# GpSimd computes twelve of the weight residues of a two-block transformer kernel

## The chip, the cores and the metric

The kernel runs on one core of a Trainium2 chip, as one program and one launch. The metric is the device time of that program in microseconds (us): 1126.8 us, the median of three runs (1125.76 to 1127.77). A core has five engines with a queue each: TensorE (PE in the rows, its weight loads PEld), VectorE (DVE), ScalarE (ACT), GpSimd (POOL) and SyncE (SP), which here only issues transfers. They work out of one on-chip memory, SBUF; the results of matmuls lie in PSUM.

## The reference, cut to what matters

Two transformer blocks follow each other on 256 rows of 1,024 features, all in float32.

```python
def first_block(x, c, ...):
    sh_m, sc_m, g_m, sh_f, sc_f, g_f = split(silu(c) @ w_ada + b_ada, 6)
    h = modulate(rmsnorm(x, norm_mix_g), sh_m, sc_m)
    q, k, v, qi, ki, wi, u, ga, gb = split(h @ w_in, split_at)
    y_attn = dsa_attention(q, k, v, qi, ki, wi) @ w_attn_proj   # top 64 keys of each row
    y_conv = conformer_conv(u, w_dw, b_dw, ln_g, ln_b) @ w_conv_proj   # 31 taps, layernorm, silu
    merged = sigmoid(ga) * y_attn + sigmoid(gb) * y_conv
    x = x + g_m * (merged @ w_out)
    a, b = split(modulate(rmsnorm(x, norm_ffn_g), sh_f, sc_f) @ w_ffn_in, 2)
    return rmsnorm(x + g_f * ((silu(a) * b) @ w_ffn_out))

def second_block(x, mem, ...):   # two attentions, cross attention to mem, feed forward
    ...
```

## The kernel before, in words

**Every product with a weight is three matmuls.** The fast float32 form of TensorE keeps fewer bits than float32, so each weight w is used as w_hi + w_lo and each activation a as a_hi + a_lo, and a product is a_hi·w_hi + a_hi·w_lo + a_lo·w_hi (`mm3`, lines 455 to 457). The weights come from memory in blocks of 1 MB into four `raw_weights` buffers (`RAW`); a block holds two *pieces* of 128x1024. For every piece ScalarE writes `w_hi` (a copy with rounding, line 909), then the residue `w_lo` = raw − w_hi is computed by VectorE (line 1223), then TensorE runs 12 matmuls of 512 columns with it. `w_hi` and `w_lo` are rings of four pieces (`RING`). The whole kernel has 277 pieces, numbered in the order of use.

**What orders a piece.** All order is written by hand: every engine runs its own list, and semaphores count. ScalarE counts `hi_ready` for each w_hi, and starts piece q when TensorE has used piece q − 4 (`piece_used`). VectorE waits for `hi_ready` ≥ q + 1 and counts `lo_ready`. TensorE waits for `lo_ready` ≥ q + 1 (`piece`, line 461 on). SyncE loads block b when `lo_ready` says that both pieces of block b − 4 are done (`load`).

**The stretch in question** holds pieces 45 to 72:

- Pieces 45 to 48 are the second slab of the first gate `ga`. Beside them VectorE runs the top-64 search: 8 rounds of `max` and `match_replace` for each half of the rows, one tap of the 31-tap convolution behind each of those (`conv_taps`, line 1407), and a residue behind every second round (pieces 45 to 52).
- Pieces 49 to 56 are the gate `gb`. Their matmuls stand inside the 16 steps of the attention, one piece in every second step (`second_gate`). A step of VectorE is a bias tile (line 1456), scores plus bias with their maximum (line 1443), its negation (line 1447), six taps, and in the odd steps from 5 on a residue (pieces 53 to 58). ScalarE takes the exponentials and turns the next w_hi. Behind the last step come the residues of pieces 59 and 60, and then the division of the attention's output (lines 1476 and 1484), the layernorm of the convolution (lines 1493 to 1557, with one small GpSimd operation, line 434) and its silu.
- Pieces 57 to 64 are the two projections of attention and convolution (`P_PA`, `P_PC`), each in two halves of the columns; VectorE multiplies their results by the gates (`gated_first` line 1514, `gated_second` lines 1522 and 1525), with two residues ahead of each such group. Pieces 65 to 72 are the output projection (`P_OUT1`).

**GpSimd** issues the transfers of `w_ada` until 162 us, each when VectorE has used the buffer (`ada_block`), and computes small reciprocal roots (`rstd`, lines 419, 434 and 444). Between 162 and 363 us it has the one operation of line 434.

## Time and profile before

| what | value |
|---|---|
| device time, median of 3 runs | 1126.8 us |
| span of the profiled execution | 1126.1 us |
| TensorE busy | 967.9 us (86%) |
| VectorE busy | 659.0 us (59%) |
| ScalarE busy | 475.3 us (42%) |
| GpSimd busy | 27.6 us (2%) |

The profile is of one execution, whose span from the first to the last instruction is 1126.1 us, 0.7 us (0.06%) below the median of the runs. The page also gives the busy share of each engine in 40 slices of 28 us. In most of them TensorE is at nine or more tenths; in the slices from 197 to 310 us, where the search and the attention lie, it falls to 8, 7, 8 and 6 while VectorE is at 8 and 9. Durations are from the first to the last cycle of an instruction; on VectorE an instruction starts some 0.08 us before the one in front of it has ended, so the distance of two starts is the cost of an instruction in a queue.

### The profile page before, as it was taken

How to read it: one execution, taken by the hardware profiler on the slowest of the kernel's cores; microseconds unless marked ns; L12 is line 12 of the kernel's file. 1: busy time of each engine (PE TensorE's matmuls, PEld its weight loads, DVE VectorE, ACT ScalarE, POOL GpSimd, SP SyncE). 2: the span in 40 equal slices, each digit the busy share in tenths (PEclk: the TensorE clock that was granted, in tenths of full speed). 3: DMA queues.
4: the chain of work that ended last, by engine and by line, in shares of the span. 5: the costliest groups of instructions: out<-in, count | busy, mean ns of one | idle time of the engine just before them, and what ended most of it. 6: DMA issues, size and time to landing. Idle time of an engine off the chain costs nothing.

```text
span 1126.1 us, 12350 instructions
## 1 busy us (share of the span) xinstructions
PE 967.9 (86%) x4205; PEld 785.5 (70%) x4205; DVE 659.0 (59%) x1074; ACT 475.3 (42%) x704; POOL 27.6 (2%) x40
## 2 busy tenths in 40 slices
PE   1998998968786999989949979876888989999896
PEld 1877886745675788878838856655677778888785
DVE  1975986899665455546655563444745355555443
ACT  3524543324434444433334434543435345555341
POOL 1110110000000000000000000000000000000000
PEclk9996996878889899999969968888999989999998
DMA  9793992412244455555714621222544044555440
GB/s 345 279 324 103 376 367 74 135 38 76 75 150 149 155 183 186 186 186 190 271 62 156 199 93 48 102 75 74 168 150 148 3 150 150 186 186 186 149 150 38
DMA packets 101541, 178.01 MB, mean 158 GB/s; under 512 B 5222, under 2 KB 51419, under 8 KB 101498
## 3 DMA queue, kind: packets, MB, share of 16 engines
q1 hardware_dynamic: 94682, 151.23, 40.6%
q0 software_dynamic: 6816, 26.22, 6.5%
q8 instruction: 25, 0.41, 0.1%
q14 instruction: 18, 0.15, 0.0%
HBM read 176.39 MB, written 1.05 MB: 158 GB/s over the span
## 4 chain that ended last, share of the span: by engine, by line
PE 52%; issue 26%; DVE 12%; ACT 5%; DMA 4%; SPq 0%; POOL 0%; DVEq 0%; POOLq 0%; ACTq 0%
PE bank L455 12%; PE bank L456 12%; PE bank L457 12%; PE bank L752 5%; DMA ada_raw<-in_w_ada 2%; DVE w_lo L1223 2%; DVE conv_out L1407 2%; ACT w_hi L909 2%; DVE ada_acc L1286 2%; DMA tap_rows<-in_w_dw 1%; PE bank L624 1%; PE bank L496 1%; PE bank L598 1%; PE bank L517 1%; PE bank L860 1%
## 5 line engine op out<-in xcount | busy, mean ns | idle before, releaser
L1223 DVE TENSOR_TENSOR w_lo<-raw_weights,w_hi 128x1024 fp32r<-128x1024 f32 x277 | 338.3, 1222 | 323.1 <-ACT w_hi L909 322.4
L909 ACT ACTIVATE w_hi<-raw_weights 128x1024 fp32r<-128x1024 f32 x277 | 292.5, 1058 | 413.0 <-PE bank L457 335.0
L455 PE MATMUL bank<-w_hi,a_hi 128*128 128x512 f32 (+1 forms) x944 | 390.0, 413 | 24.5 <-DVE a_lo L1738 6.0
L456 PE MATMUL bank<-w_lo,a_hi 128*128 128x512 f32 (+1 forms) x944 | 381.8, 404 | 0.0
L457 PE MATMUL bank<-w_hi,a_lo 128*128 128x512 f32 (+1 forms) x944 | 381.2, 404 | 0.0
L455 PEld LDWEIGHTS bank<-w_hi,a_hi 128*128 128x128 f32 x944 | 189.0, 200 | 71.8 <-issue 30.6
L457 PEld LDWEIGHTS bank<-w_hi,a_lo 128*128 128x128 f32 x944 | 187.9, 199 | 40.6
L456 PEld LDWEIGHTS bank<-w_lo,a_hi 128*128 128x128 f32 x944 | 188.9, 200 | 37.5
L1286 DVE SCALAR_TENSOR_TENSOR ada_acc<-ada_raw,row_stats,ada_acc 128x512 f32<-128x512 f32 (+1 forms) x84 | 62.9, 749 | 6.6 <-DMA ada_raw<-in_w_ada 4.8
L752 PE MATMUL bank<-w_hi,ff_hi 128*128 128x512 f32 x176 | 56.2, 401 | 6.3 <-DVE hidden_rows L1579 3.2
L752 PE MATMUL bank<-w_lo,ff_hi 128*128 128x512 f32 x176 | 55.5, 397 | 0.0
L752 PE MATMUL bank<-w_hi,ff_lo 128*128 128x512 f32 x176 | 55.4, 396 | 0.0
L1407 DVE SCALAR_TENSOR_TENSOR conv_out<-conv_in,conv_taps_T,conv_out 128x256 f32<-128x256 f32 x120 | 50.8, 475 | 0.0
L752 PEld LDWEIGHTS bank<-w_hi,ff_hi 128*128 128x128 f32 x176 | 33.4, 191 | 14.4 <-DVE hidden_rows L1579 3.6
L752 PEld LDWEIGHTS bank<-w_lo,ff_hi 128*128 128x128 f32 x176 | 33.9, 193 | 7.2
L752 PEld LDWEIGHTS bank<-w_hi,ff_lo 128*128 128x128 f32 x176 | 33.9, 192 | 7.2
L1056 ACT ACTIVATE probabilities_T<-bank 128x128 f32<-128x128 f32 (+1 forms) x32 | 10.6, 330 | 39.8 <-PE bank L633 39.8
L517 PE MATMUL bank<-constants,z_projected 128*128 128x128 f32 x88 | 17.1, 368 | 11.3 <-DVE z_projected L1646 3.9
L506 PE MATMUL bank<-constants,x_residual 128*128 128x128 f32 x48 | 9.8, 390 | 18.8 <-DVE x_residual L1622 12.7
L1443 DVE CUSTOM_DVE_ANT_0 masked_scores<-bank,bias_tile 128x128 f32<-128x128 f32 (+1 forms) x32 | 11.5, 358 | 24.4 <-issue 12.4
L413 POOL DMA_DIRECT2D ada_raw<-in_w_ada x24 | 18.1, 757 | 303.4 <-DVE ada_acc L1286 294.7
L1048 ACT ACTIVATE probabilities<-masked_scores,row_stats 128x128 f32<-128x128 f32 (+1 forms) x32 | 14.4, 450 | 25.9 <-DVE row_stats L1447 25.7
(218 smaller groups left out, 699.3 us busy)
## 6 DMA issues: line engine op xcount, KB each, us to landing
raw_weights<-in_w_in SPq DMA_DIRECT2D x40, 1024.0 KB, 5.1
ada_raw<-in_w_ada POOLq DMA_DIRECT2D x24, 1024.0 KB, 6.4
raw_weights<-in_w_ffn_in SPq DMA_DIRECT2D x44, 512.0 KB, 4.3
raw_weights<-in_w_gate_up SPq DMA_DIRECT2D x44, 512.0 KB, 4.3
raw_weights<-in_w_ffn_out SPq DMA_DIRECT2D x9, 1024.0 KB, 5.0
raw_weights<-in_w_down SPq DMA_DIRECT2D x9, 1024.0 KB, 5.0
raw_weights<-in_w_ckv SPq DMA_DIRECT2D x8, 1024.0 KB, 11.4
raw_weights<-in_w_out SPq DMA_DIRECT2D x8, 1024.0 KB, 5.0
```

The lines of the kernel that those rows point to most:

```text
L413: pool.dma_start(ada_raw[:, n % 2, :].rearrange("p (k n) -> p k n", k=4), slab_src(w2["w_ada"], 4 * k, s)).then_inc(ada_landed[n % 2], 16)
L455: pe.matmul(ps, hi[:, kt, ts], wh, start=start, stop=False)
L456: pe.matmul(ps, hi[:, kt, ts], wl, start=False, stop=False)
L457: return pe.matmul(ps, lo[:, kt, ts], wh, start=False, stop=stop)
L517: last = pe.transpose(bank[b0 + g][:, kk * SEQ + t * P:kk * SEQ + (t + 1) * P], src[:, t, c:c + P], ident)
L752: last = pe.matmul(bank[2 * t + c][:], lhs[:, kt, ts], w[:, c * W:(c + 1) * W], start=(kt == 0 and n == 0), stop=(kt == KF - 1 and n == 2))
L909: act.activation(w_hi[:, q % RING, 0:m], raw[:, b % RAW, half * PIECE:half * PIECE + m], ACT.Copy)\
L1048: act.activation(p_work[:, n % 2, 0, 0:keys], s_work[:, n % 2, 0, 0:keys], ACT.Exp, bias=stat[:, 34 + n % 2:35 + n % 2], accum_out=stat[:, ...
L1223: dve.tensor_tensor(w_lo[:, q % RING, 0:m], raw[:, b % RAW, half * PIECE:half * PIECE + m], w_hi[:, q % RING, 0:m], ALU.subtract).then_inc ...
L1286: o = dve.scalar_tensor_tensor(out=slot, in0=w, scalar=c, in1=slot, op0=ALU.mult, op1=ALU.add)
L1407: dve.scalar_tensor_tensor(out=conv_out[:, g, :], in0=conv_in[:, g, k:k + SEQ], scalar=taps[:, g, k:k + 1], in1=conv_out[:, g, :], op0=ALU ...
L1443: dve.tensor_tensor_reduce(s_work[:, n % 2, 0, 0:keys], bank[4 + n % 2][:, 0:keys], bias, DH ** -0.5, -3e38, ALU.add, ALU.max, stat[:, 32 ...
```

## The change

`POOL_LO` is a list of twelve pieces: 46, 48, 50, 52, 54, 56, 58, 60, 62, 64, 66 and 68. VectorE leaves their residues out; GpSimd computes them, each when `hi_ready` says that w_hi is there, and counts a semaphore of its own, `pool_lo`. Whoever waits for a residue (TensorE's `piece`, SyncE's `load`) waits for `pool_lo` for these pieces and for `lo_ready` for all others, whose counts are lower by the pieces that were left out before them. A block of which one piece is GpSimd's has two waits ahead of its load. For that the loads of blocks 21 to 28 are written out in place of a loop. The subtraction itself, its operands and the rings are the same.

```diff
+POOL_LO = tuple(range(P_IN1 + 29, P_OUT1 + 4, 2))
+
+def lo_before(p):
+    return p - sum(q < p for q in POOL_LO)
...
+    def lo_event(p):
+        return (pool_lo, POOL_LO.index(p) + 1) if p in POOL_LO else (lo_ready, lo_before(p) + 1)
...
             if b >= RAW:
-                sp.wait_ge(lo_ready, last_piece_of(b - RAW) + 1 + i * step)
+                q = last_piece_of(b - RAW)
+                if q in POOL_LO or q - 1 in POOL_LO:
+                    sp.wait_ge(*lo_event(q - 1))
+                    sp.wait_ge(*lo_event(q))
+                else:
+                    sp.wait_ge(lo_ready, lo_before(q) + 1 + i * step)
...
+        def residue(q):
+            b, half = block_of(q)
+            pool.wait_ge(hi_ready, q + 1)
+            pool.tensor_tensor(w_lo[:, q % RING, :], raw[:, b % RAW, half * PIECE:(half + 1) * PIECE],
+                               w_hi[:, q % RING, :], ALU.subtract).then_inc(pool_lo, 1)
+        for q in POOL_LO:
+            if q < P_PC:
+                residue(q)
         pool.wait_ge(sem["ln_var"], 1)
         pool.tensor_tensor(stat[:, 62:64], ..., ALU.pow).then_inc(sem["ln_rstd"], 1)
+        for q in POOL_LO:
+            if q >= P_PC:
+                residue(q)
         rstd(N_H2)
...
         def piece(p, u, j, n, i=0, ...):
-            pe.wait_ge(lo_ready, p + 1 + i * 8)
+            ready_sem, count = lo_event(p)
+            pe.wait_ge(ready_sem, count + i * 8)
...
         def conv(p, n=1, i=0):        # VectorE
             for q in range(p, p + n):
+                if q in POOL_LO:
+                    continue
```

**VectorE in the top-64 search.** `MAX` and `MATCH_REPLACE` are the two steps of a round, and `conv_out<-conv_in,conv_taps_T,conv_out` is a tap. Before, a residue stands behind every second round:

```order
L1423 MATCH_REPLACE score<-top_75,score 128x256 [waits top_step]
L1407 SCALAR_TENSOR_TENSOR conv_out<-conv_in,conv_taps_T,conv_out 128x256 [waits conv_done]
L1223 TENSOR_TENSOR w_lo<-raw_weights,w_hi 128x1024 [waits hi_ready]
L1420 MAX top_75<-score 128x8 [waits top_step]
L1407 SCALAR_TENSOR_TENSOR conv_out<-conv_in,conv_taps_T,conv_out 128x256 [waits conv_done]
```

Now, where the piece is GpSimd's:

```order
L1458 MATCH_REPLACE score<-top_75,score 128x256 [waits top_step]
L1442 SCALAR_TENSOR_TENSOR conv_out<-conv_in,conv_taps_T,conv_out 128x256 [waits conv_done]
L1455 MAX top_75<-score 128x8 [waits top_step]
L1442 SCALAR_TENSOR_TENSOR conv_out<-conv_in,conv_taps_T,conv_out 128x256 [waits conv_done]
L1458 MATCH_REPLACE score<-top_75,score 128x256 [waits top_step]
```

The residue and its wait for `hi_ready` are gone between the two rounds; four of the eight residues of the search go in this way (pieces 46, 48, 50 and 52).

**The end of the attention, VectorE and GpSimd.** `RECIPROCAL` and the two operations behind it divide the attention's output. VectorE before:

```order
L1407 SCALAR_TENSOR_TENSOR conv_out<-conv_in,conv_taps_T,conv_out 128x256 [waits conv_done] x2
L1223 TENSOR_TENSOR w_lo<-raw_weights,w_hi 128x1024 [waits hi_ready] x3
L1476 RECIPROCAL row_stats<-row_stats 128x16 [waits attention_exp]
L1484 TENSOR_TENSOR z_projected<-bank,row_stats 128x512 [waits attention_pv,attention_recip]
L1484 TENSOR_TENSOR z_projected<-bank,row_stats 128x512
L1493 TENSOR_TENSOR conv_out<-conv_out,bank 128x1024 [waits ln_mean]
```

VectorE now:

```order
L1442 SCALAR_TENSOR_TENSOR conv_out<-conv_in,conv_taps_T,conv_out 128x256 [waits conv_done] x2
L1258 TENSOR_TENSOR w_lo<-raw_weights,w_hi 128x1024 [waits hi_ready]
L1511 RECIPROCAL row_stats<-row_stats 128x16 [waits attention_exp]
L1519 TENSOR_TENSOR z_projected<-bank,row_stats 128x512 [waits attention_pv,attention_recip]
L1519 TENSOR_TENSOR z_projected<-bank,row_stats 128x512
L1528 TENSOR_TENSOR conv_out<-conv_out,bank 128x1024 [waits ln_mean]
```

GpSimd before, from the last issue of `w_ada` of the loop on:

```order
L413 DMA ada_raw<-in_w_ada 128x4x512
L429 REGISTER_ALU
L429 COMPARE_AND_BRANCH
L434 TENSOR_TENSOR row_stats<-row_stats,constants 128x2 [waits ln_var]
L419 TENSOR_TENSOR row_stats<-row_stats,constants 128x2 [waits norm_mean]
```

GpSimd now:

```order
L432 DMA ada_raw<-in_w_ada 128x4x512
L448 REGISTER_ALU
L448 COMPARE_AND_BRANCH
L456 TENSOR_TENSOR w_lo<-raw_weights,w_hi 128x1024 [waits hi_ready] x8
L463 TENSOR_TENSOR row_stats<-row_stats,constants 128x2 [waits ln_var]
L456 TENSOR_TENSOR w_lo<-raw_weights,w_hi 128x1024 [waits hi_ready] x4
L438 TENSOR_TENSOR row_stats<-row_stats,constants 128x2 [waits norm_mean]
```

Of the three residues ahead of the division (58, 59, 60) one stays (59). GpSimd has eight residues ahead of the layernorm's small operation, which stands in a queue behind the one of piece 60, and four behind it.

**VectorE at the second gating.** Before, with the two halves of the columns:

```order
L1223 TENSOR_TENSOR w_lo<-raw_weights,w_hi 128x1024 [waits hi_ready] x2
L1522 TENSOR_TENSOR z_projected<-bank,z_projected 128x512 [waits piece_used]
L1525 TENSOR_TENSOR z_projected<-z_projected 128x512 [waits acc0_free]
L1522 TENSOR_TENSOR z_projected<-bank,z_projected 128x512
L1525 TENSOR_TENSOR z_projected<-z_projected 128x512 [waits acc1_free]
```

Now:

```order
L1258 TENSOR_TENSOR w_lo<-raw_weights,w_hi 128x1024 [waits hi_ready]
L1557 TENSOR_TENSOR z_projected<-bank,z_projected 128x512 [waits piece_used]
L1560 TENSOR_TENSOR z_projected<-z_projected 128x512 [waits acc0_free]
L1557 TENSOR_TENSOR z_projected<-bank,z_projected 128x512
L1560 TENSOR_TENSOR z_projected<-z_projected 128x512 [waits acc1_free]
```

One residue in place of two stands ahead of each group (65 ahead of the first half, 67 ahead of the second).

## Rows read from the trace of the kernel before

**Rows 1.** The page: the span, and busy time of each engine.

```profile
span 1126.1 us, 12350 instructions
PE 967.9 (86%) x4205; PEld 785.5 (70%) x4205; DVE 659.0 (59%) x1074; ACT 475.3 (42%) x704; POOL 27.6 (2%) x40
```

**Rows 2.** Windows: busy us (instructions) by engine, granted clock, DMA share, GB/s.

```profile
215.20:231.00 15.80, 7.35 (x33) 5.75 (x32) 15.71 (x41) 5.43 (x6) 0.00 (x0) 0.80 0.26 77
231.00:291.00 60.00, 49.52 (x200) 36.21 (x200) 57.07 (x164) 24.04 (x60) 0.00 (x0) 0.82 0.16 55
291.00:303.00 12.00, 7.50 (x38) 6.57 (x37) 6.87 (x11) 5.54 (x7) 0.71 (x1) 0.73 0.43 158
```

**Rows 3.** The page's costliest groups: count, busy us, mean ns, idle before, releaser.

```profile
L1223 DVE TENSOR_TENSOR w_lo<-raw_weights,w_hi 128x1024 fp32r<-128x1024 f32 x277 | 338.3, 1222 | 323.1 <-ACT w_hi L909 322.4
L909 ACT ACTIVATE w_hi<-raw_weights 128x1024 fp32r<-128x1024 f32 x277 | 292.5, 1058 | 413.0 <-PE bank L457 335.0
L1407 DVE SCALAR_TENSOR_TENSOR conv_out<-conv_in,conv_taps_T,conv_out 128x256 f32<-128x256 f32 x120 | 50.8, 475 | 0.0
```

**Rows 4.** Timeline of the search's second half: start us, us, engine, what.

```profile
215.22 1.22 DVE L1223 TENSOR_TENSOR w_lo<-raw_weights,w_hi 128x1024 fp32r<-128x1024 f32 x1 [3.30 <-ACT w_hi L909]
216.36 0.42 DVE L1420 MAX8 top<-score 128x8 f32<-128x256 f32 x1
216.70 0.47 DVE L1407 SCALAR_TENSOR_TENSOR conv_out<-conv_in,conv_taps_T,conv_out 128x256 f32<-128x256 f32 x1
...
217.21 1.06 ACT L909 ACTIVATE w_hi<-raw_weights 128x1024 fp32r<-128x1024 f32 x1 [2.02 <-PE bank L457]
...
231.01 1.61 PE L624 MATMUL bank<-kT,qT 64*128 64x128 f32 x4 [8.46 <-DVE modulation_T L1373]
```

**Rows 5.** Timeline inside the attention, VectorE and TensorE.

```profile
258.70 1.22 DVE L1223 TENSOR_TENSOR w_lo<-raw_weights,w_hi 128x1024 fp32r<-128x1024 f32 x1
...
275.33 0.29 DVE L1443 CUSTOM_DVE_ANT_0 masked_scores<-bank,bias_tile 128x128 f32<-128x128 f32 x1
...
266.65 0.69 PE L633 MATMUL bank<-constants,probabilities 128*128 128x128 f32 x2 [2.67 <-ACT probabilities L1048]
...
273.58 0.48 PE L624 MATMUL bank<-kT,qT 64*128 64x128 f32 x2
```

**Rows 6.** Timeline of the attention's end, VectorE and TensorE.

```profile
291.83 1.23 DVE L1223 TENSOR_TENSOR w_lo<-raw_weights,w_hi 128x1024 fp32r<-128x1024 f32 x1 [1.30 <-ACT w_hi L909]
293.26 1.29 DVE L1484 TENSOR_TENSOR z_projected<-bank,row_stats 128x512 f32<-128x512 f32 x2
295.71 1.22 DVE L1496 TENSOR_TENSOR conv_sq<-conv_out 128x1024 f32<-128x1024 f32 x1
...
290.49 0.78 PE L640 MATMUL bank<-z_projected,probabilities_T 128*128 128x64 f32 x6
...
302.21 1.19 PE L691 MATMUL bank<-conv_sq,constants 128*128 128x256 f32 x2 [1.65 <-DVE conv_sq L1505]
```

**Rows 7.** Timeline of the second gating, VectorE, ScalarE and TensorE.

```profile
322.57 1.23 DVE L1223 TENSOR_TENSOR w_lo<-raw_weights,w_hi 128x1024 fp32r<-128x1024 f32 x1 [1.50 <-ACT w_hi L909]
...
328.01 1.22 DVE L1223 TENSOR_TENSOR w_lo<-raw_weights,w_hi 128x1024 fp32r<-128x1024 f32 x1 [0.43 <-ACT w_hi L909]
...
326.92 1.06 ACT L909 ACTIVATE w_hi<-raw_weights 128x1024 fp32r<-128x1024 f32 x1 [1.66 <-PE bank L457]
...
331.95 1.97 PE L704 MATMUL bank<-constants,z_projected 128*128 128x128 f32 x8 [4.25 <-DVE z_projected L1525]
```

**Rows 8.** Groups of instructions: count, busy us, mean ns, idle before, releaser.

```profile
L419 POOL TENSOR_TENSOR row_stats<-row_stats,constants 128x2 f32<-128x2 f32 x8 | 5.6, 702 | 455.6 <-DVE row_stats L1231 450.3 <-DMA constants<-shape_constants 5.3
...
L1447 DVE TENSOR_SCALAR row_stats<-row_stats 128x1 f32<-128x1 f32 x32 | 4.9, 154 | 1.2 <-DVE row_stats L1443 0.2
...
L1235 DVE TENSOR_SCALAR scaled_rows<-x_residual,row_stats 128x1024 f32<-128x1024 f32 x1 | 0.8, 753 | 0.8 <-POOL row_stats L419 0.8
...
L1525 DVE TENSOR_TENSOR z_projected<-z_projected 128x512 f32<-128x512 f32 x8 | 5.5, 692 | 0.3
```

More of the change, by code:

```diff
@@ L224, in build @@
     hi_ready, lo_ready, piece_used = S("hi_ready"), S("lo_ready"), S("piece_used")
+    pool_lo = S("lo_by_gpsimd")
+    def lo_event(p):
+        return (pool_lo, POOL_LO.index(p) + 1) if p in POOL_LO else (lo_ready, lo_before(p) + 1)
     acc_free = [S("acc0_free"), S("acc1_free")]
@@ L344, in _ @@
                 load(13 + j, slab_src(w2["w_in"], 4 * (j % 2), i * (2 * W) + (j // 2) * W), None, i, 8)
-        with sp.Fori(0, 2) as i:
-            for j in range(4):
-                load(21 + j, slab_src(w2["w_in"], 4 * (j % 2), i * (2 * W) + (C_GA + (j // 2) * W)), None, i, 8)
+        for s in range(4):
+            for j in range(2):
+                load(21 + 2 * s + j, slab_src(w2["w_in"], 4 * j, C_GA + s * W))
         sp.dma_start(final_g[:], a["norm_final_g"].partition_broadcast(P)).then_inc(final_landed, 16)
@@ L552, in _ @@
         turn(N_H1, xs_z)
-        pe.wait_ge(lo_ready, P_SMALL + 1)
+        pe.wait_ge(*lo_event(P_SMALL))
         for t in range(TT):
@@ L744, in feed_forward @@
                     reduce_gate(8 * 12, gate_slot).then_inc(sem["ada_reduced"], 1)
-                pe.wait_ge(lo_ready, p + kt + 1)
+                pe.wait_ge(*lo_event(p + kt))
                 pe.wait_ge(*after(tag, "hidden_lo", kt // 2 + 1))
```

## The prediction

> **What bounds the kernel now.** I read the page first: TensorE is busy for 86% of 1126.1 us and VectorE for 59% [rows 1], so over the whole kernel taking work from VectorE buys nothing: w_lo has 323.1 us of idle time before it, nearly all of it waiting for ScalarE's w_hi [rows 3], and w_hi in turn waits for TensorE. The windows show where that is otherwise. From 215.2 us, where VectorE's last wait in the search ends, to 231.0 VectorE is busy for 15.71 of 15.80 us and TensorE for 7.35; from 231 to 291, in the attention, VectorE is busy for 57.07 of 60 us [rows 2]. The timeline says the same from the other side: TensorE's first scores at 231.01 had waited 8.46 us for VectorE [rows 4]. So from 215 to 293 us the list of VectorE is the path. From 303 to 326.7 TensorE runs without a gap and nothing is to be had, and at 331.95 it has waited 4.25 us for the second gating [rows 7]. What the change is worth is read from these places alone.
>
> **What is taken from VectorE.** Twelve residues of 1.22 us [rows 3], 14.7 us of busy time; in a queue one costs the distance of two starts, 216.36 − 215.22 = 1.14 us [rows 4]. Piece by piece:
> - 46, 48, 62 and 64 lie where VectorE waits anyway: ahead of 215.22 it had stood idle for 3.30 us until TensorE had used piece 45 [rows 4]. Nothing is gained, and a delay of VectorE by up to 3.3 + 2 × 1.14 = 5.6 us ahead of 215 is covered.
> - 50 and 52, in the second half of the search: 2 × 1.14 = 2.3 us, all on the path. The rounds need no w_hi, and that of piece 51 is there early enough.
> - 54 and 56 lie behind the steps of the attention: 2.3 us. What is late next is TensorE: the scores for the step of 275.33 were ready at 273.58 + 0.48 = 274.06, 1.27 us ahead of it, while TensorE itself had stood for 2.67 us at 266.65 waiting for the exponential, which moves with VectorE [rows 5]. I take 2.0 us, with 1.3 and 2.3 as ends.
> - 58 and 60 at the end. Behind 58 VectorE stood idle, so its absence there frees nothing. 60 starts at 291.83, after 1.30 us of waiting for its w_hi, and the division starts at 293.26. Without it the division waits for the attention's last matmuls, over at 290.49 + 0.6 = 291.1, and for its reciprocal, 0.3 us: 291.4, a gain of 1.85 us, handed through the layernorm to TensorE at 302.21 [rows 6].
> - 66 and 68: without 66 (322.57) the first half of the gating starts when TensorE has used piece 62, some 2 us earlier; the second half then waits for piece 64, used at 326.92 (ScalarE's w_hi is released by it), and not for the residue of 68, which ends at 328.01 + 1.14 = 329.15 [rows 7]. That is 329.15 − 326.95 = 2.2 us of the 4.25.
>
> Together 2.3 + 2.0 + 1.85 + 2.2 = 8.3 us, if GpSimd's work is free.
>
> **What is put on GpSimd.** The trace has no operation of this size on it. Its nearest row, 128x2, takes 702 ns where VectorE takes 154 for 128x1 [rows 8]; by that factor of 4.6 a residue would take 5.6 us, which is the upper end, and 1.22, VectorE's own, is the lower. I take 2.4, twice VectorE's, for an engine that reads its two operands one after the other; ScalarE passes one operand of this size in 1.06 [rows 3], and two such passes are 2.1. As a price from a page alone: the Trainium skill (GPSIMD Engine Reference, Performance versus the Vector engine) gives 4,497 ns for a float32 `tensor_tensor` of 2,048 elements, which would be an estimate of 2.25 us here and change the sum by under 1 us.
>
> At 2.4 us nobody waits for the result itself. In the projections w_hi of piece q ends 1.1 us after TensorE has used piece q − 4, and three pieces of 2.72 us lie between (the distance of two w_hi there, 1.06 + 1.66 [rows 7]): 8.2 − 1.1 = 7.1 us for the residue. In the search and the attention the distance is longer. The small operation of the layernorm stands behind piece 60's residue, which is over 5 us ahead of it. SyncE's two waits per block are eight pieces ahead of the use. The loads written out without a loop cost nothing: its queue waits on residues.
>
> **What it costs VectorE.** This decides the case, and no row shows it: nowhere does GpSimd read SBUF beside a VectorE operation with two operands there. What rows do show is that VectorE with one operand of 128x1024 in SBUF takes 0.753 us and with two 1.22 [rows 3, 8]. With one operand it goes at twice the rate per element, so a second way into SBUF exists, and two operands fill both. If GpSimd reads through one of them, the two engines must take turns whenever VectorE has two operands in SBUF, and that is a tap (0.475 us, 120 of them [rows 3]), a bias tile and a residue: most of the stretch. The bounds: no hold at all, or the whole 2.4 us of GpSimd's operation less what VectorE has to do meanwhile with one operand. I put turn-taking ahead, for the doubled rate is what a shared second way would look like. The Trainium skill (SBUF — State Buffer, Who interferes with whom) states this outright: a VectorE instruction with two SBUF inputs contends with a GpSimd instruction that reads SBUF, and the later one is blocked until the first has finished. By that rule the sum is the one that follows, and without it 8.3 us are gained.
>
> The sum with turns:
> - 50 and 52: each holds the next tap for 2.4 less a `MAX` or `MATCH_REPLACE` of 0.35, against 1.14 saved: 2 × (2.05 − 1.14) = +1.8.
> - 54 and 56: 2.4 less up to 0.75 of one-operand work (scores and negation), so 1.65 to 2.4 against 1.14: +0.5 to +1.3 each; I take +0.9, so +1.8.
> - 58: its w_hi comes in the taps ahead of the last step, so it holds them for nothing to 2.4, and nothing is saved there: +1.2.
> - 60: the division reads one operand from PSUM and goes on; the square at 295.71 [rows 6], two operands, loses some 0.4: −1.85 + 0.4 = −1.4.
> - 66 and 68: the operations of line 1525 have two operands in SBUF (0.692 us [rows 8]) and meet both: of the 2.2 us some 0.5 is left, −0.5.
> - 46, 48, 62 and 64: held inside idle time, 0.
>
> +1.8 + 1.8 + 1.2 − 1.4 − 0.5 = **+2.9 us**, a span of 1129.0 and, with the 0.7 between span and median, 1129.7. With the friendly end of each term the sum is 0, with the other +6.
>
> **The rivals.**
> - *Side by side.* The engines read without touching each other. Then the price is 0 and all of 8.3 us stays: 1118.5, between 1116.5 and 1120.5 with the ends of the attention term and with TensorE's clock, which was granted at 0.82 of full in the attention [rows 2] and may rise a little when it waits less. For it speaks that a row that would contradict it is missing; against it the doubled rate. This is the case of the other side; it decides from the point where a residue holds VectorE for under about 74% of what I assume (8.3 of 11.2 us), as with an operation of under 2.0 us.
> - *GpSimd waits for gaps.* VectorE's taps follow without a pause, and GpSimd gets in only at scores, `MAX` and idle time. Then the holds are at their friendly ends and gain and loss cancel: 1126.8, from 1125 to 1128.5.
> - *The long operation.* Turns, and a residue of 5.6 us: five holds on the path each 3.2 us longer, 16 us more: about 1145. Above 5.4 us (two pieces of 2.72) GpSimd would also fall behind TensorE in the projections. Nothing but the factor of tiny operations speaks for it.
>
> **How the numbers follow.** Turns 0.56, of which 0.35 slower by over 0.2% (2.3 us, about what a measurement of this kernel can tell from no change), 0.20 within and 0.01 faster; side by side 0.33, faster; gaps 0.06, within; long operation 0.05, slower. Faster 0.34, same 0.26, slower 0.40. The range has to reach both main cases, 1117.5 to 1133; outside it lie the long operation and the tails of the two. The likeliest case's own range is 1126.5 to 1133.
>
> **What would show it.** A residue of GpSimd of 2.2 to 2.6 us when nothing is beside it. With turns, taps or `MAX`-separated taps that last, or stand, 1.5 to 2.4 us longer exactly once per GpSimd residue, the first scores at about 232.8 in place of 231.01, and the division at about 296; side by side, taps all at 0.475, the first scores near 228.7 and the division near 287. In both, the wait of 4.25 ahead of TensorE's turn of the second half shrinks: to 2.0 side by side, to about 3.8 with turns. From 340 us on the rest should be the same with a shift. The prediction is wrong if taps keep their length beside a GpSimd residue, if that residue takes under 2 us, or if TensorE is seen waiting for `pool_lo`.

## The result, and the profile after

The changed kernel takes 1130.7 us (median of 5 runs, 1129.3 to 1131.2) against 1126.6 us for the kernel before (5 runs, 1124.7 to 1127.8). The ratio is 1.0032, with an interval of 1.0018 to 1.0045: slower by 4.1 us, where 2.9 were forecast. The engines take turns.

The page of the changed kernel answers to [rows 1]. Its group lines give count, busy us, mean ns, idle time ahead and its releaser:

```profile
span 1128.4 us, 12333 instructions
PE 965.2 (86%) x4205; PEld 783.3 (69%) x4205; DVE 660.9 (59%) x1062; ACT 474.7 (42%) x704; POOL 58.0 (5%) x52
...
L1258 DVE TENSOR_TENSOR w_lo<-raw_weights,w_hi 128x1024 fp32r<-128x1024 f32 x265 | 323.7, 1223 | 318.0 <-ACT w_hi L942 317.4
...
L456 POOL TENSOR_TENSOR w_lo<-raw_weights,w_hi 128x1024 fp32r<-128x1024 f32 x12 | 30.5, 2539 | 136.1 <-ACT w_hi L942 136.1
```

VectorE has twelve instructions less, 323.7 us of residues in place of 338.3, and yet it is busy for 1.9 us *more*. So its other instructions grew by 14.6 + 1.9 = 16.5 us. The group of the taps, from 190 to 340 us, says which:

```profile
L1442 DVE SCALAR_TENSOR_TENSOR conv_out<-conv_in,conv_taps_T,conv_out 128x256 f32<-128x256 f32 x120 | 63.8, 583 | 0.0
```

Before, the same 120 took 50.8 us [rows 3]: 13.0 us more. Most of the rest, 2.9 us, is in two additions of the second gating, shown below. The timeline of the search shows one of them, VectorE and then GpSimd (start us, us, engine, what):

```profile
213.25 1.22 DVE L1258 TENSOR_TENSOR w_lo<-raw_weights,w_hi 128x1024 fp32r<-128x1024 f32 x1
...
215.18 0.41 DVE L1458 MATCH_REPLACE8 score<-top,score 128x256 f32<-128x256 f32 x1
215.51 2.23 DVE L1442 SCALAR_TENSOR_TENSOR conv_out<-conv_in,conv_taps_T,conv_out 128x256 f32<-128x256 f32 x1
217.66 0.41 DVE L1455 MAX8 top<-score 128x8 f32<-128x256 f32 x1
```

```profile
214.99 2.46 POOL L456 TENSOR_TENSOR w_lo<-raw_weights,w_hi 128x1024 fp32r<-128x1024 f32 x1 [7.52 <-ACT w_hi L942]
```

`MATCH_REPLACE`, with one operand in SBUF, passes beside GpSimd in its usual 0.41 us. The tap behind it begins at 215.51 and ends at 217.74, 0.29 us after GpSimd has ended (214.99 + 2.46 = 217.45). Without GpSimd it takes 0.47.

An operand in PSUM does not meet GpSimd either. The residue of piece 60 lies beside the division's multiplications and the first step of the layernorm, each with one operand in SBUF and one in PSUM (`bank`), and the latter takes its usual 1.22 us (GpSimd and VectorE):

```profile
297.26 2.37 POOL L456 TENSOR_TENSOR w_lo<-raw_weights,w_hi 128x1024 fp32r<-128x1024 f32 x1 [8.47 <-ACT w_hi L942]
...
298.46 1.22 DVE L1528 TENSOR_TENSOR conv_out<-conv_out,bank 128x1024 f32<-128x1024 f32 x1 [0.42 <-PE bank L702]
```

In the attention, one step's six taps (2.45 us before) and the last step's taps, with the step between on which VectorE waits for scores (the row names the bias tile, but that was over 0.75 us earlier; TensorE's scores ended at 276.04):

```profile
252.12 4.53 DVE L1442 SCALAR_TENSOR_TENSOR conv_out<-conv_in,conv_taps_T,conv_out 128x256 f32<-128x256 f32 x6
...
276.53 0.29 DVE L1478 CUSTOM_DVE_ANT_0 masked_scores<-bank,bias_tile 128x128 f32<-128x128 f32 x1 [0.74 <-DVE bias_tile L1491]
...
284.53 4.54 DVE L1442 SCALAR_TENSOR_TENSOR conv_out<-conv_in,conv_taps_T,conv_out 128x256 f32<-128x256 f32 x6
```

The end of the attention, TensorE and then VectorE, answers to [rows 6]:

```profile
290.75 0.69 PE L666 MATMUL bank<-constants,probabilities 128*128 128x128 f32 x2 [4.41 <-ACT probabilities L1081]
...
292.51 0.63 PE L487 MATMUL bank<-w_hi,a_hi 128*128 128x512 f32 x1
...
295.87 0.78 PE L673 MATMUL bank<-z_projected,probabilities_T 128*128 128x64 f32 x6
```

```profile
292.83 1.23 DVE L1258 TENSOR_TENSOR w_lo<-raw_weights,w_hi 128x1024 fp32r<-128x1024 f32 x1 [1.98 <-ACT w_hi L942]
293.98 0.25 DVE L1511 RECIPROCAL row_stats<-row_stats 128x16 f32<-128x16 f32 x1
296.75 1.29 DVE L1519 TENSOR_TENSOR z_projected<-bank,row_stats 128x512 f32<-128x512 f32 x2 [2.53 <-PE bank L673]
```

The residue of piece 60 is gone, and still the division starts 3.5 us later than before: it waits 2.53 us for TensorE, which is late by the attention, and whose piece 56 takes 4.8 us in place of 2.8. And the second gating, VectorE and TensorE [rows 7]:

```profile
326.10 2.18 DVE L1560 TENSOR_TENSOR z_projected<-z_projected 128x512 f32<-128x512 f32 x1
...
330.21 0.69 DVE L1560 TENSOR_TENSOR z_projected<-z_projected 128x512 f32<-128x512 f32 x1
...
331.54 2.12 DVE L1560 TENSOR_TENSOR z_projected<-z_projected 128x512 f32<-128x512 f32 x1
```

```profile
333.71 1.97 PE L737 MATMUL bank<-constants,z_projected 128*128 128x128 f32 x8 [3.39 <-DVE z_projected L1560]
```

**By stages.** From such rows every profiled execution was cut at five points: (a) VectorE starts the residue of piece 49, (b) TensorE starts the first scores, (c) the maximum of the attention's last step is read, (d) the division starts, (e) TensorE starts the turn of the second half, then the end of the span. Distances in us:

| kernel | a to b | b to c | c to d | d to e | e to end |
|---|---|---|---|---|---|
| before | 15.79 | 55.50 | 6.75 | 38.69 | 794.2 |
| changed | 17.03 | 59.51 | 6.96 | 36.96 | 794.7 |
| e_search | 17.39 | 55.45 | 8.34 | 38.68 | 794.2 |
| e_attn | 15.80 | 59.54 | 8.36 | 38.50 | 794.3 |
| e_end | 15.79 | 55.53 | 4.90 | 38.57 | 792.2 |
| e_noread | 13.53 | 53.13 | 6.33 | 37.16 | 790.2 |
| e_beside0 | 15.79 | 55.52 | 6.75 | 38.71 | 794.2 |
| e_beside1 | 17.02 | 57.87 | 9.04 | 39.01 | 794.3 |
| e_beside2 | 19.72 | 61.80 | 6.76 | 40.65 | 791.7 |
| e_quarters | 14.63 | 57.72 | 6.16 | 35.47 | 791.7 |
| e_early | 17.02 | 59.59 | 4.22 | 38.69 | 792.4 |
| e_reorder | 15.79 | 55.52 | 4.90 | 37.15 | 794.0 |
| e_both | 15.79 | 55.52 | 2.64 | 36.45 | 789.4 |
| e_both_quarters | 14.81 | 55.40 | 2.75 | 37.15 | 787.6 |

The first two columns repeat to 0.2 us wherever the kernels agree there (0.4 for e_search, whose list from a to b is the changed kernel's), and they carry the argument. The last column differs by some 4 us between kernels that are alike behind (e) (all but the last three), so a whole time is read from the runs and not from one profile. Two profiled executions lie well off their kernel's median: that of e_search took 1135.2 us (8.4 above it), that of e_quarters 1119.0 (4.2 below it).

### The profile page after: what moved, and what is told of

Its sections match the earlier page's. It is cut to its first block, busy times and chain, and to the rows that moved or that the text cites. A ratio compares the mean times of both kernels' runs of the same rounds, so it can differ in the third digit from the quotient of the medians.

```text
span 1128.4 us, 12333 instructions
## 1 busy us (share of the span) xinstructions
PE 965.2 (86%) x4205; PEld 783.3 (69%) x4205; DVE 660.9 (59%) x1062; ACT 474.7 (42%) x704; POOL 58.0 (5%) x52
## 4 chain that ended last, share of the span: by engine, by line
PE 52%; issue 24%; DVE 14%; ACT 5%; DMA 4%; POOL 1%; SPq 0%; DVEq 0%; POOLq 0%; ACTq 0%
PE bank L487 13%; PE bank L488 12%; PE bank L489 12%; PE bank L785 5%; DVE conv_out L1442 3%; DMA ada_raw<-in_w_ada 3%; DVE w_lo L1258 2%; ACT w_hi L942 2%; DVE ada_acc L1321 2%; DMA tap_rows<-in_w_dw 1%; PE bank L657 1%; PE bank L529 1%; PE bank L550 1%; PE bank L631 1%; PE bank L893 1%
## 5 line engine op out<-in xcount | busy, mean ns | idle before, releaser
L1258 DVE TENSOR_TENSOR w_lo<-raw_weights,w_hi 128x1024 fp32r<-128x1024 f32 x265 | 323.7, 1223 | 318.0 <-ACT w_hi L942 317.4
L1442 DVE SCALAR_TENSOR_TENSOR conv_out<-conv_in,conv_taps_T,conv_out 128x256 f32<-128x256 f32 x120 | 63.8, 583 | 0.0
L456 POOL TENSOR_TENSOR w_lo<-raw_weights,w_hi 128x1024 fp32r<-128x1024 f32 x12 | 30.5, 2539 | 136.1 <-ACT w_hi L942 136.1
L432 POOL DMA_DIRECT2D ada_raw<-in_w_ada x24 | 18.1, 756 | 302.9 <-DVE ada_acc L1321 294.2
L666 PE MATMUL bank<-constants,probabilities 128*128 128x128 f32 x48 | 13.4, 339 | 16.6 <-ACT probabilities L1081 16.4
L438 POOL TENSOR_TENSOR row_stats<-row_stats,constants 128x2 f32<-128x2 f32 x8 | 5.6, 702 | 426.2 <-DVE row_stats L1266 420.7
```

The source lines that it names most:

```text
L432: pool.dma_start(ada_raw[:, n % 2, :].rearrange("p (k n) -> p k n", k=4), slab_src(w2["w_ada"], 4 * k, s)).then_inc(ada_landed[n % 2], 16)
L456: pool.tensor_tensor(w_lo[:, q % RING, :], raw[:, b % RAW, half * PIECE:(half + 1) * PIECE], w_hi[:, q % RING, :], ALU.subtract).then_inc( ...
L666: last = pe.transpose(bank[6][:, kt * P:(kt + 1) * P], p_work[:, n % 2, 0, kt * P:(kt + 1) * P], ident)
L1258: dve.tensor_tensor(w_lo[:, q % RING, 0:m], raw[:, b % RAW, half * PIECE:half * PIECE + m], w_hi[:, q % RING, 0:m], ALU.subtract).then_inc ...
L1442: dve.scalar_tensor_tensor(out=conv_out[:, g, :], in0=conv_in[:, g, k:k + SEQ], scalar=taps[:, g, k:k + 1], in1=conv_out[:, g, :], op0=ALU ...
```

## The experiments

### Each part alone

```diff
-POOL_LO = tuple(range(P_IN1 + 29, P_OUT1 + 4, 2))
+POOL_LO = (46, 48, 50, 52)          # e_search
+POOL_LO = (54, 56, 58)              # e_attn
+POOL_LO = (60, 62, 64, 66, 68)      # e_end
```

e_search: 

> GpSimd computes the residues of pieces 46, 48, 50 and 52 only; VectorE computes all others. Turns theory: in the search each residue of GpSimd stretches one tap by 1.8 to 1.9 us; the two ahead of the idle time cost nothing, the other two cost 2 x 1.76 and save 2 x 1.14, so the time is 1.2 us above before (+0.1%). Rival, side by side (the loss of the whole change lies elsewhere, for instance in TensorE's clock): 2.3 us below before.

e_attn: 

> GpSimd computes the residues of pieces 54, 56 and 58 only. Turns theory: each stretches the taps by 1.5 to 2.1 us, two save 1.14 each and the third saves nothing, and TensorE, which then waits over 4 us ahead of piece 56, runs that piece at its lower clock (4.8 in place of 2.85 us): 4 to 6 us above before. Without the effect of the clock 3 to 4 us above. Rival, side by side: 2 us below.

e_end: 

> GpSimd computes the residues of pieces 60, 62, 64, 66 and 68 only. Turns theory: piece 60 gives 1.85 less 0.4 us, the gating gives 0.9 us of its 2.2 (one addition in each half is stretched from 0.69 to 2.1 us): 2.3 us below before, faster by 0.2%. Side by side: 4 us below. If GpSimd's residues cost everywhere: at or above before.

Measured, as ratios to the kernel before: e_search 1.0005 (0.9991 to 1.0019), e_attn 1.0046 (1.0033 to 1.0058), e_end 0.9967 (0.9954 to 0.9979): +0.6, +5.2 and -3.7 us, each with about 1.5 us of uncertainty, +2.1 together against +3.6 by the ratio of the whole. In its own stage e_search costs 1.6 us and e_attn 4.0, as the changed kernel does within 0.4. The rest of e_attn's loss lies between (c) and the division (8.36 against 6.75), where TensorE waits 4.83 us and the first half of piece 56 runs at the low clock. By the whole time e_search is not told from no change, while "side by side", 2.3 us below, is outside its interval. In e_end the division comes 1.85 us sooner (6.75 to 4.90), which is the forecast's gain for piece 60 to the digit, since there TensorE's last wait is what it was:

```profile
287.79 0.44 PE L666 MATMUL bank<-constants,probabilities 128*128 128x128 f32 x2 [2.75 <-ACT probabilities L1081]
```

So the change is a gain where VectorE has few two-operand instructions beside the residue, and a loss where the taps follow each other.

### Is it GpSimd's reading?

Three kernels put twelve operations on GpSimd beside the kernel *before*, at the pieces of `POOL_LO`, on data that nobody waits for (two resident operands of 128x1024, one, none):

```diff
+        def beside(q):
+            pool.wait_ge(hi_ready, q + 1)
...
+            pool.tensor_tensor(dst, mem_v[:, :, 0:W], mem_v[:, :, W:2 * W], ALU.subtract)   # e_beside2
+            pool.tensor_scalar(dst, mem_v[:, :, 0:W], 1.0, None, ALU.mult)                  # e_beside1
+            pool.memset(dst, 0.0)                                                           # e_beside0
```

e_beside2: 

> The kernel before with all its residues on VectorE; GpSimd in addition subtracts two 128x1024 operands of resident data into a place that nobody reads, twelve times, at the moments at which it computes a residue in the change. Turns theory: nothing is saved and every hold stays, 2 x 1.8 in the search, 1.5 to 2.1 for each of 54, 56 and 58, about 1.4 for each of 66 and 68, some clock: 11 to 14 us above before (1.0 to 1.2%). Side by side: no difference.

e_beside1: 

> The same with an operation of one operand (a multiplication by 1) in place of two. Turns theory: the taps are held again, each as long as this shorter operation lasts; if it lasts 1.0 to 1.3 us, 3 to 6 us above before. If only two reading streams of GpSimd get in the way: no difference.

e_beside0: 

> The same with an operation that only writes (a fill with zeros). If what is shared is the way in which an engine reads: no tap is stretched and the time is that of before within 0.2%. If any GpSimd operation on SBUF holds VectorE: each tap beside it is stretched by its duration, 3 to 5 us above before.

A fourth is the changed kernel in which GpSimd only fills `w_lo`, so that TensorE's a_hi·w_lo of twelve pieces is that of a constant:

```diff
-            pool.tensor_tensor(w_lo[:, q % RING, :], raw[...], w_hi[:, q % RING, :], ALU.subtract).then_inc(pool_lo, 1)
+            pool.memset(w_lo[:, q % RING, :].bitcast(F32), 0.0).then_inc(pool_lo, 1)
```

e_noread: 

> The change with GpSimd filling w_lo with zeros in place of subtracting: VectorE has the same list as in the change, but GpSimd reads nothing, so the part a_hi times w_lo of these twelve pieces is left out. Turns in reading only: no hold is left and the whole of the gain shows that I worked out for work that is free on GpSimd, 8.3 us below before (0.7%). If the gain was overrated (TensorE or ScalarE next in line): 3 to 6 us below. If writes hold too: near before.

Measured: e_beside2 1.0110 (1.0078 to 1.0143), e_beside1 1.0051 (1.0037 to 1.0064), e_beside0 1.0006 (0.9996 to 1.0016), e_noread 0.9917 (0.9900 to 0.9933), that is +12, +6, +0.7 and -9.3 us. The first, the third and the fourth came as the theory had them; in e_beside1 the time is in the expected range, but the operation lasts 3.34 us in the mean and not 1.0 to 1.3 (last section). The groups between 190 and 340 us, of e_beside2, e_beside0 and e_noread in this order:

```profile
L1419 DVE SCALAR_TENSOR_TENSOR conv_out<-conv_in,conv_taps_T,conv_out 128x256 f32<-128x256 f32 x120 | 64.7, 591 | 0.0
...
L438 POOL TENSOR_TENSOR z_projected<-mem_v 128x1024 f32<-128x1024 f32 x12 | 34.7, 2892 | 138.6 <-ACT w_hi L921 138.6
```

```profile
L1419 DVE SCALAR_TENSOR_TENSOR conv_out<-conv_in,conv_taps_T,conv_out 128x256 f32<-128x256 f32 x120 | 50.9, 476 | 0.0
...
L438 POOL MEMSET z_projected<- 128x1024 f32 x12 | 11.4, 954 | 147.2 <-ACT w_hi L921 147.2
```

```profile
L1442 DVE SCALAR_TENSOR_TENSOR conv_out<-conv_in,conv_taps_T,conv_out 128x256 f32<-128x256 f32 x120 | 50.9, 476 | 0.0
...
L456 POOL MEMSET w_lo<- 128x1024 f32 x12 | 11.4, 954 | 144.3 <-ACT w_hi L941 144.3
```

An operation that reads holds the taps though nobody uses its result, one that only writes does not (476 ns). In e_beside1, where GpSimd reads one operand, the taps take 514 ns in the mean. This shows that the price is the reading, and neither the waits nor the semaphores that the change adds. e_noread is also the rival "side by side" made real: 2.26 us gained in the search and 2.37 in the attention, where 2.3 and 2.0 had been worked out. From (c) to (e), however, it gains 1.95 and not 4.05: half of piece 56 ran at the low clock there too, after a wait of 2.70 us. So the whole, 9.3 against 8.3, is nearer to the forecast than its parts are. The Trainium skill (SBUF — State Buffer, SBUF: two separate sides) has it that the two engines lock a shared pair of ports for a whole instruction, VectorE with two SBUF inputs only against a GpSimd operation that reads. The four runs agree on who holds whom. On "for a whole instruction" the two-operand operation agrees and e_beside1 does not: it holds a tap for 0.75 of its 2.77 us.

### Turns by the instruction: the residue in quarters

```diff
-            pool.tensor_tensor(w_lo[:, q % RING, :], raw[...], w_hi[:, q % RING, :], ALU.subtract).then_inc(pool_lo, 1)
+            for c in range(half * PIECE, (half + 1) * PIECE, 256):
+                o = c - half * PIECE
+                pool.tensor_tensor(w_lo[:, q % RING, o:o + 256], raw[:, b % RAW, c:c + 256],
+                                   w_hi[:, q % RING, o:o + 256], ALU.subtract).then_inc(pool_lo, 1)
```

e_quarters: 

> The changed kernel, with every residue of GpSimd written as four operations of 128x256 in place of one of 128x1024. If the two engines take turns by whole instructions, no tap is held for more than about 0.7 us, but four are held for each residue in place of one: the sum of the taps' extra time stays near 9 us or grows by GpSimd's fixed cost, and the time is 0 to +3 us against the changed kernel (ratio to the kernel before 1.003 to 1.006). If a hold came from something that lasts as long as GpSimd has work at all, single taps would still last 2.2 us or more. If the engines shared the way cycle by cycle, the taps would all grow by the same small share, and nothing would change with the size.

Measured: 0.9965 (0.9949 to 0.9981), 1123.2 us. This is 7.5 us *below* the changed kernel, and faster than the kernel before. The expectation was wrong: I had let four short holds add up to one long one. The groups of this kernel between 190 and 340 us, a stretch of the search, and GpSimd and VectorE at the residue of 58:

```profile
L1444 DVE SCALAR_TENSOR_TENSOR conv_out<-conv_in,conv_taps_T,conv_out 128x256 f32<-128x256 f32 x120 | 57.3, 528 | 0.0
L458 POOL TENSOR_TENSOR w_lo<-raw_weights,w_hi 128x256 fp32r<-128x256 f32 x48 | 40.1, 864 | 121.4 <-ACT w_hi L944 121.4
```

```profile
214.52 0.79 DVE L1444 SCALAR_TENSOR_TENSOR conv_out<-conv_in,conv_taps_T,conv_out 128x256 f32<-128x256 f32 x1
215.23 0.08 DVE L1460 MATCH_VALUE_LOAD score<-top,score 128x8 f32 x1
215.31 0.40 DVE L1460 MATCH_REPLACE8 score<-top,score 128x256 f32<-128x256 f32 x1
215.63 0.56 DVE L1444 SCALAR_TENSOR_TENSOR conv_out<-conv_in,conv_taps_T,conv_out 128x256 f32<-128x256 f32 x1
```

```profile
281.35 3.42 POOL L458 TENSOR_TENSOR w_lo<-raw_weights,w_hi 128x256 fp32r<-128x256 f32 x4 [12.01 <-ACT w_hi L944]
...
279.71 2.92 DVE L1444 SCALAR_TENSOR_TENSOR conv_out<-conv_in,conv_taps_T,conv_out 128x256 f32<-128x256 f32 x6
282.55 0.94 DVE L1493 SCALAR_TENSOR_TENSOR bias_tile<-constants,score 128x256 f32<-128x256 f32 x1
...
284.06 1.37 DVE L1444 SCALAR_TENSOR_TENSOR conv_out<-conv_in,conv_taps_T,conv_out 128x256 f32<-128x256 f32 x2
```

GpSimd works longer (40.1 us against 30.5), but the taps grow by 6.5 us in place of 13.0. Between two quarters VectorE gets in, and in the search part of each quarter lies beside `MAX` and `MATCH_REPLACE`. In the attention the four quarters of a residue hold only three instructions, for about 0.5 us each: here a tap in the run of six (2.92 in place of 2.45), the bias tile (0.94 in place of 0.42) and a tap in the run of two (1.37 in place of 0.87); one quarter falls beside the scores, which have one operand in SBUF. That is 1.5 us in place of the 2.08 of a whole residue. Against e_noread, where nothing is held, a whole residue costs (17.03 - 13.53) / 2 = 1.75 us in the search and (59.51 - 53.13) / 3 = 2.13 in the attention, and one in quarters 0.55 and 1.53. VectorE's own costs 1.14. That is the rule of the case: in quarters it pays in the search and not in the attention. By the stages the two stretches with taps account for 4.2 of the 7.5 us below the changed kernel. Another 2.3 lie between (c) and (e): the held additions of the second gating take 1.21 and 1.19 us in place of 2.18 and 2.12, and TensorE's wait at (e) is 2.56 in place of 3.39. Against the kernel before, the stages give 1.2 us won in the search, 2.2 lost in the attention and 3.8 won from (c) to (e), TensorE's clock included.

### TensorE's piece behind the last wait

```diff
             for n in range(len(STEPS)):
+                ahead = between is not None and n == len(STEPS) - 1
+                if ahead:
+                    between(n // 2)
                 turn_p(n)
...
-                if between is not None and n % 2:
+                if between is not None and n % 2 and not ahead:
                     between(n // 2)
```

e_early: 

> The changed kernel, with one difference: TensorE runs the attention's last gate piece (56) ahead of the last step's turn instead of behind it. In the changed kernel TensorE waits 4.41 us ahead of that turn (290.75), then runs piece 56 at the lower of its two clocks until 295.87, and the division waits for it 2.53 us, until 296.75. Theory (the end of the attention lost its gain because the piece stood behind a longer wait): the piece goes into the wait, runs in 2.8 us, the division starts 2.5 us sooner, at about 294.2, where VectorE is free for it, and the time is some 2.5 us below that of the changed kernel (ratio to the kernel before about 1.001). Rival (VectorE's taps and the residue of 59 are what set the division, and TensorE's clock is of no weight): the division stays within 0.5 us of 296.75 and the time with it (ratio about 1.003).

Measured: 1.0009 (0.9998 to 1.0020), 1127.9 us, 2.8 us below the changed kernel. TensorE and VectorE of this kernel:

```profile
291.08 0.44 PE L666 MATMUL bank<-constants,probabilities 128*128 128x128 f32 x2 [1.63 <-ACT probabilities L1084]
```

```profile
294.34 1.29 DVE L1522 TENSOR_TENSOR z_projected<-bank,row_stats 128x512 f32<-128x512 f32 x2
```

From (c) to the division it is 4.22 us in place of 6.96, as expected (the division at 294.34, 294.2 expected), and VectorE waits for nobody there. But the path gives back 1.73 us between the division and (e) (38.69 against 36.96), where TensorE's clock is lower than in the changed kernel: granted at 0.68 of full from 294.3 to 303.7, against 0.82 there. By the profiles the piece's place is thus worth 1 us until (e); by the runs it is 2.6 ± 2.0. That it sets the division is shown; how much of the whole it is worth is not settled closer than that.

### What VectorE can do alone

If the residues on the path are the matter, they can be moved in VectorE's own list to where it waits, without GpSimd. e_reorder does that to the kernel before:

```diff
-        conv(P_IN1 + 42, 2)
+        conv(P_IN1 + 42)
...                                  # behind the a_lo of the attention's output
+        conv(P_IN1 + 43)
...                                  # second gating, in both blocks
-                conv(p2 + 4 + 2 * c, 2)
+                conv(p2 + 4 + 2 * c)
...                                  # behind the addition that ends the half
+                conv(p2 + 5 + 2 * c)
```

e_reorder: 

> No residue on GpSimd. VectorE computes piece 60's residue behind the layernorm's square and the attention's a_lo, and of each pair ahead of the second gating the second one behind it, in both blocks. Theory: what the change gains at these places is the place in VectorE's queue, not the engine: 1.85 + 2.2 us in the first block and 2.2 in the second, 6 us below before (0.5%). Rival: the residues are late for TensorE or ScalarE there and nothing is gained; or only the first block gains, 4 us.

e_both adds the order of e_early, moves piece 59 the same way, and in the second block

```diff
-        conv(P_IN2 + 42, 2)
+        conv(P_IN2 + 42)
...                                  # behind the scaling of the attention's rows
+        conv(P_IN2 + 43)
```

e_both: 

> No residue on GpSimd. As the kernel in which VectorE computes residues 60, 66 and 68 of the first block (and their counterparts of the second) later in its own list, and three moves more: piece 56 ahead of the last turn on TensorE, residue 59 beside 60 behind the attention's a_lo, and the last residue of the second block's differential attention behind the scaling of its rows, where VectorE waits 6.2 us. In the kernel it builds on, the division waits for TensorE until 289.92 and could start at about 287.6: -2.1 us; the copies of the second block's rows start at 770.88 after a wait of 1.33 us and a residue of 1.15, while TensorE's values are over at 769.1: -1.7 us. With the -5.4 us measured for that kernel this makes about -9 us against the kernel before, ratio 0.992. If ScalarE's function table loads (1.28 us each) set both places instead, only -6 to -7 us.

e_both_quarters adds `POOL_LO = (46, 48, 50, 52)` with the residue in quarters:

e_both_quarters: 

> The fastest kernel so far (residues 59, 60, 66 and 68 later in VectorE's own list, piece 56 ahead of the last turn, the second block's residue moved), and the residues of 46, 48, 50 and 52, those of the top-64 search, on GpSimd, each as four operations of 128x256. If a residue in quarters holds VectorE in the search for the 0.56 us that the kernel with quarters shows (14.63 us from the residue of 49 to the first scores, against 13.5 without any hold), the stretch from the residue of 49 to the first scores goes from 15.79 us to 14.6: about -1.2 us against that kernel, ratio 0.989 against the kernel before. If that kernel's gain came from one fortunate execution and a quarter costs what a whole residue costs per element (4 x 0.44 = 1.75), the stretch is 17.0 us and the time +1.2, ratio 0.9915.

Measured: e_reorder 0.9949 (0.9934 to 0.9964), 1121.4 us; e_both 0.9904 (0.9889 to 0.9919), 1116.4 us; e_both_quarters 0.9881 (0.9863 to 0.9899), 1115.2 us. Expected were 0.995, 0.992 and 0.989: e_both gained 1.8 us more than that, and the last interval leaves out its rival, 0.9915. In e_both the division and, in the second block, the copies of the rows start when TensorE is done (in the kernel before the copies, at 776.08, stood behind a residue that had waited 1.33 us for its w_hi):

```profile
286.38 1.29 DVE L1486 TENSOR_TENSOR z_projected<-bank,row_stats 128x512 f32<-128x512 f32 x2 [0.28 <-PE bank L640]
...
764.28 1.67 DVE L1729 COPY z_projected<-bank 128x128 f32<-128x128 f32 x8 [0.85 <-PE bank L811]
```

The last kernel's stretch from (a) to (b) is 14.81 us, against 14.6 expected and 15.79 without GpSimd. The stage shows that gain; the two intervals of the whole overlap. So of the kernel's 13 us some 1 is GpSimd's work in the search, and 11 come from the order of the instructions. The residues of the second gating and of the end of the attention were not tried on GpSimd in that kernel.

## Why the prediction was right, and where it was not

**GpSimd's residue, 2.4 us.** Measured 2.54 in the mean and 2.37 for the shortest. The long end of 5.6 is out.

**Turns.** The tap of 215.51 is the row that was forecast, and the number fits: 13.0 us over the seven residues that lie among the taps, 1.86 each. "GpSimd waits for gaps" is out by the same row, where GpSimd is inside its operation and the tap stands, and "side by side" by e_noread, which is 12.5 us faster than the changed kernel with the same waits and the same list on VectorE. The argument for turns was thinner than its result: the two rows compared, 0.753 and 1.22 us, are 1.6 times apart. It is twice per element only beyond a fixed part (128x256 takes 0.40 us with one operand, `TENSOR_SCALAR` in the kernel before, and 0.475 with two). And a faster VectorE operation could not show that GpSimd uses the same way; the runs beside it did.

**50 and 52, +1.8.** From (a) to (b) it is +1.24. The step was right and the hold too long: 1.75 us in place of 2.05. The tap starts 0.52 us into the residue, where I had taken 0.35, and ends 0.29 us behind it, which is less than the 0.47 it takes alone.

**54 and 56, +1.8; 58, +1.2.** From (b) to (c) it is +4.0 in place of 3.0. The mis-sized term is 58, for which I took the middle of 0 and 2.4: the six taps of 284.53 take 4.54 in place of 2.46, +2.08. GpSimd starts it at 286.17, 0.33 us ahead of the last of the six taps, and nothing covers the hold. 54 and 56 cost the rest, 1.9, of which 0.74 is VectorE's wait for scores at 276.53 that I had named as what is late next. Its margin was smaller than the 1.27 us that I gave it: the scores end at 276.04 and VectorE starts 0.49 later, so of the 1.27 some 0.8 were left.

**60, -1.4; 66 and 68, -0.5.** From (c) to (e) it is -1.5 us in the changed kernel and -2.0 in e_end, against -1.9. The sum holds, the way to it does not, and that it holds is in part luck. In e_end the division gains the whole 1.85: the square is not held (1.23 us; GpSimd's residue, 292.24 to 294.60, is over before it), so the 0.4 for it was wrong. But from the division to (e) e_end gains only 0.12. VectorE waits 0.42 us for TensorE ahead of line 1528, and the gating gives 0.36 of the 0.5 (from the layernorm's last turn on TensorE to (e), 29.38 in place of 29.74). In the changed kernel nothing is gained at the division (6.96 against 6.75). TensorE had waited 4.41 us ahead of the last turn, and then most of piece 56 ran at 1.2 GHz (matmuls of 0.63 us; at 2.4 GHz they take 0.39), until 295.07. Before, after a wait of 2.75, it ran at 2.4 GHz. The gain reappears behind the division, where the granted clock is 0.82 from the division to the layernorm's last turn on TensorE (296.75 to 305.23), against 0.68 before (293.26 to 302.21). The prediction had no term for that clock, though piece 56 stood on the path to the division; it was not the wait's length alone either, for in e_search the piece ran at the low clock after a wait of 1.97. The cause of the clock in each of these is open.

**46, 48, 62 and 64, 0.** For 46 and 48 this holds only while TensorE is slow ahead of piece 49. The cover was the wait of 3.30 us [rows 4], and it comes from pieces that ran mostly at the low clock (granted 0.58 from 207.0 to 215.2). In the changed kernel they ran at the high one (1.00 from 205.0 to 213.25), and VectorE came to (a) without any wait. That the change brings the high clock is not shown: e_attn has it there too, with the list of the kernel before up to (a). e_attn, with the same clock there and no GpSimd in the search, takes 20.36 us from its first `MAX` (193.40) to (a) and waits 0.41; the changed kernel takes 21.30 (191.95 to 213.25). So where the cover is gone the two holds cost 0.9 us. The prediction gave the cover but not the case without it.

**The sum.** 1.24 + 4.01 - 1.52 = +3.7 by the stages, up to +4.7 with the uncovered 0.9, and +4.1 by the medians. **The offset** between the span and a median, 0.7 us, was the wrong way to link the two. An execution of the kernel before takes 1.6 to 1.75 us more than its span (65 executions, beside the experiments), so the one profiled, with a span of 1126.1, took about 1127.8 and stood 1.2 us above its kernel's median. The changed kernel's five executions take 1.9 to 2.1 more than their spans. So from median to median the span grows by some 3.7 us, as the stages say, and 0.3 to 0.4 of the 4.1 lie outside the span, for which the runs show no cause. In the forecast's own terms the span came out 0.6 us short of 1129.0 and the offset 1.6 too small (2.3 in place of 0.7).

**The signs.** GpSimd's residue, the taps held once for each of the residues among them, and the division (296.75, about 296 forecast) came as described. TensorE never waits for `pool_lo`. The first scores are at 230.28 and not at 232.8, because (a) itself came 2.0 us earlier in this execution. The wait at (e) shrank to 3.39 us, further than to 3.8.

## What to carry to other kernels

Before elementwise work goes from VectorE to GpSimd, look at what VectorE runs beside it: if those instructions have two operands in SBUF, most of GpSimd's duration is VectorE's loss, and the residue that took 1.2 us costs 1.8 to 2.1. If it must go there, cut it into short operations and lay them beside instructions with one operand, or let GpSimd only write. And first ask whether the work can stand later in VectorE's own list, behind the instruction that the path waits for: here such moves, one of TensorE's among them, were worth 11 us where the change lost 4.

## What the runs showed of the hardware

The hold goes both ways. GpSimd's longest residue began 0.18 us behind one of VectorE, and took 3.24 us, 0.87 more than the shortest. In e_beside2 the five operations that start just behind a residue of VectorE take 3.22 to 3.45 us, the seven others 2.34 to 2.63. The changed kernel, VectorE and GpSimd:

```profile
204.05 1.21 DVE L1258 TENSOR_TENSOR w_lo<-raw_weights,w_hi 128x1024 fp32r<-128x1024 f32 x1
```

```profile
204.23 3.24 POOL L456 TENSOR_TENSOR w_lo<-raw_weights,w_hi 128x1024 fp32r<-128x1024 f32 x1 [2.88 <-ACT w_hi L942]
```

With one operand GpSimd is shown no faster than with two: 2.77 to 3.81 us in e_beside1 (mean 3.34) against 2.34 to 3.45 in e_beside2. But it holds VectorE for far less of that. In e_beside1, GpSimd and VectorE:

```profile
216.45 2.77 POOL L438 TENSOR_SCALAR z_projected<-mem_v 128x1024 f32<-128x1024 f32 x1 [10.55 <-ACT w_hi L921]
```

```profile
216.55 1.22 DVE L1419 SCALAR_TENSOR_TENSOR conv_out<-conv_in,conv_taps_T,conv_out 128x256 f32<-128x256 f32 x1
...
218.09 0.47 DVE L1419 SCALAR_TENSOR_TENSOR conv_out<-conv_in,conv_taps_T,conv_out 128x256 f32<-128x256 f32 x1
```

The first tap is held for 0.75 us, and the second, also inside GpSimd's span, not at all. The Trainium skill (GPSIMD Engine Reference, Engine selection) has it that on GpSimd "1-input is roughly line-rate"; this trace, with VectorE at work beside it, shows 2.77 us at the least against VectorE's 0.753 [rows 8] and doesn't agree, while a fill of the same size, which reads nothing, takes 0.95. The next operation (221.88, 2.77 us) lets go at the same point: the held tap of each ends 1.32 us after GpSimd's start (217.77 and 223.20). Why a one-operand operation lasts so long and yet lets go early was not tried.
